# First attention of a two-block transformer kernel: bias row inside the keys, output projection and two value units among the heads, identity transposes in TensorE's waits

## The reference, cut to what matters

```python
u = rms_norm(h, norm_mix[0]); m = rms_norm(mem, norm_mem[0])
mk, mv = split(m @ w_mem_kv[0])
q, k, v, f_logit, mq = split(u @ fox_w_in)        # 12 heads of 64; mq: 4 heads
q = rms_norm(q, g_q); k = rms_norm(k, g_k)        # per head
c = cumsum(log_sigmoid(f_logit + b_f))
s = q @ k.T / 8 + (c[t] - c[s]);  s = where(causal, s, -1e30)
mix = softmax(s) @ v                              # forget ("fox") attention
mem_out = softmax(rms_norm(mq) @ rms_norm(mk).T / 8) @ mv
h = h + concat(mix, mem_out) @ fox_w_out          # 1024 x 1024
h = h + swiglu(rms_norm(h))                       # FFN
```

## Time and profile before

| | |
|---|---|
| time, median of 3 runs | 1890.23 us (1889.27 to 1890.61) |
| the profiled execution | 1889.91 us |
| its span, first to last instruction | 1888.1 us |
| PE busy | 1796.5 us (95%) |
| DVE / ACT / POOL busy | 77% / 62% / 11% |
| share of the chain that ended last | PE 85%, DVE 6%, ACT 5%, issue 2% |
| mean granted PE clock | 0.988 |

### The profile page before, as it was taken

The page is one execution under the profiler, slowest core; times in us unless marked ns, Lnnn a source line. Parts: engine busy times, 40 slices in busy tenths (PEclk is TensorE's granted clock), DMA queues, the critical chain, the costliest instruction groups (busy, mean ns, idle before and its releaser), DMA issues.

```text
span 1888.1 us, 27534 instructions
## 1 busy us (share of the span) xinstructions
PE 1796.5 (95%) x10586; PEld 1578.9 (84%) x10586; DVE 1446.0 (77%) x1327; ACT 1169.4 (62%) x1135; POOL 207.5 (11%) x161
## 2 busy tenths in 40 slices
PE   6988999999999999999999999999999999689997
PEld 5977999999878878788787887878877888589997
DVE  6765877779768888888888888888889854765554
ACT  5535444356667777877777778787776734743332
POOL 2033111122020000000000000000015000302221
PEclk8999999999999999999999999999999999899999
DMA  9604688841259999999999999999999933035540
GB/s 395 244 23 146 232 335 329 315 184 55 112 219 383 378 363 385 348 402 373 368 387 359 389 385 362 379 358 394 377 356 410 369 112 135 1 135 179 182 154 23
DMA packets 74571, 520.84 MB, mean 276 GB/s; under 512 B 8064, under 2 KB 8192, under 8 KB 13952
## 3 DMA queue, kind: packets, MB, share of 16 engines
q1 hardware_dynamic: 73056, 514.02, 71.7%
q0 software_dynamic: 1440, 5.77, 0.8%
HBM read 504.02 MB, written 15.73 MB: 275 GB/s over the span
## 4 chain that ended last, share of the span: by engine, by line
PE 85%; DVE 6%; ACT 5%; issue 2%; DMA 1%; POOL 1%; ACTq 0%; DVEq 0%; SPq 0%
PE ps L1174 25%; PE ps L1176 25%; PE ps L1175 25%; DVE wl L1688 2%; PE ps L1197 1%; ACT wh L1048 1%; PE ps L1375 1%; PE ps L1543 1%; DMA raw<-in_experts 1%; PE ps L1305 1%; PE ps L1326 1%; DVE sqz L1681 1%; ACT L1059 0%; ACT L1048 0%; PE ps L1188 0%
## 5 line engine op out<-in xcount | busy, mean ns | idle before, releaser
L1688 DVE TENSOR_TENSOR wl<-raw,wh 128x2048 fp32r<-128x2048 f32 x446 | 1025.9, 2303 | 294.5 <-ACT wh L753 169.2
L1048 ACT ACTIVATE wh<-raw 128x2048 fp32r<-128x2048 f32 x336 | 643.2, 1918 | 180.2 <-PE ps L1176 177.0
L1174 PE MATMUL ps<-wh,xh 128*128 128x512 f32 (+1 forms) x1040 | 397.9, 383 | 8.9 <-DVE wl L1688 8.8
L1176 PE MATMUL ps<-wh,xl 128*128 128x512 f32 (+1 forms) x1040 | 390.1, 375 | 0.0
L1175 PE MATMUL ps<-wl,xh 128*128 128x512 f32 (+1 forms) x1040 | 389.7, 375 | 0.0
L1174 PE MATMUL ps<-xh,wh 128*128 128x256 f32 x1184 | 343.4, 290 | 25.1 <-DVE xl L1688 11.4
L1175 PE MATMUL ps<-xl,wh 128*128 128x256 f32 x1184 | 338.9, 286 | 0.0
L1176 PE MATMUL ps<-xh,wl 128*128 128x256 f32 x1184 | 338.6, 286 | 0.0
L753 ACT ACTIVATE wh<-raw 128x2048 fp32r<-128x2048 f32 x107 | 204.2, 1909 | 175.0 <-PE ps L1176 171.1
L1174 PEld LDWEIGHTS ps<-xh,wh 128*128 128x128 f32 x1184 | 231.3, 195 | 30.2 <-issue 23.8
L1174 PEld LDWEIGHTS ps<-wh,xh 128*128 128x128 f32 x1040 | 195.9, 188 | 49.8 <-DVE wl L1688 15.9
(11 more groups left out here) (292 smaller groups left out, 1927.9 us busy)
## 6 DMA issues: line engine op xcount, KB each, us to landing
raw<-in_experts SPq DMA_DIRECT2D x336, 1024.0 KB, 6.9
raw<-in_units SPq DMA_DIRECT2D x134, 1024.0 KB, 6.0
x_rows<-big SPq DMA_DIRECT2D x1, 6144.0 KB, 34.5
big<-x_rows SPq DMA_DIRECT2D x8, 512.0 KB, 8.2
y_rows<-big SPq DMA_DIRECT2D x7, 512.0 KB, 8.3
y_rows<-big SPq DMA_DIRECT2D x1, 2560.0 KB, 40.4
big<-in_mem SPq DMA_DIRECT2D x1, 1024.0 KB, 7.1
hT<-in_x SPq DMA_DIRECT2D x1, 1024.0 KB, 9.0
```

What stands on the lines that cost most here:

```text
L1048: act.activation(wh[:, p % SPL, :], raw[:, n % RAW, :], ACT.Copy).then_inc(sem("hi_ready"), 1)
L1174: mm(out_, lh, rh, start=start, stop=False, **kw)
L1176: return mm(out_, ll, rh, start=False, stop=stop, **kw)
L1688: return V.tensor_tensor(out_, whole, leading.bitcast(F32), ALU.subtract)
```

## The change

1. The bias goes into the keys. Row 64 of an even head's `kz`, and row 0 of an odd head's, were zero; two DMAs issued by POOL put -c there. The matching row of the queries holds ones: queries of odd heads go to a new buffer `q_odd`, and POOL sets rows with four memsets. The 24 matmuls of L1308, `selh` and its copy go away; a query unit is scaled with two 64x512 instructions.
2. The order of units becomes fq0 fk0 fq1 fk1 fq2 fk2 fv0; fv1 and fv2 are multiplied in quarters (`values_half`) at steps 0 to 2 of the attention, and copied out by ACT at steps 2 and 3.
3. The output projection is stored by rows and added up in banks 4 to 7 as pairs finish: `fo_rows(g)`, 24 matmuls, at the even steps from 8 to 18, the last two behind the loop. Turned probabilities (bank 2) and pair outputs (bank 3) have one bank each now.
4. ACT copies turned probabilities first and takes exponentials after, and writes `xh` one step earlier; DVE's `xl` stays where it was. fo0 is split ahead of the attention, and `FOX_SPLITS` puts the splits of fo1, fo2, fo3 and of the first two FFN units at steps 6, 9, 11, 15 and 19.
5. PE transposes the identity into an unused bank at five waits (16, 16, 20, 20 and 20 times) and 12 times ahead of each pair in stick-breaking.

```diff
-UNITS_A = (["mk0", "mv0", "mq0"] + [f"{w}{j}" for w in ("fq", "fk", "fv") for j in range(3)]
+PROJ = ["fq0", "fk0", "fq1", "fk1", "fq2", "fk2", "fv0"]
+UNITS_A = (["mk0", "mv0", "mq0"] + PROJ + ["fv1", "fv2"]
...
-        selh = sqz[:, 0:FOX_HEADS * P].rearrange("p (h m) -> p h m", h=FOX_HEADS)
-        negc = sqz[:, FOX_HEADS * P:FOX_HEADS * P + T]
+        q_odd = view(0, FOX // P, T, sqz)
+        negc = plan_f[:, :, :].rearrange("p a b -> p (a b)")
...
-        FOX_SPLITS = {16: ("fv0",), 20: ("fv1", "fv2")}
+        FOX_SPLITS = {6: ("fv1",), 9: ("fv2",), 11: ("fo0",), 15: ("fo1",), 19: ("fo2",)}
...
-        add_attention(fox_maps)
+        add_attention(fox_maps, (2,), (3,))
         for j in range(4):
-            product(f"fo{j}", j)
-        S.add("nsum2", 6)
+            product(f"fo{j}", 4 + j)
+        S.add("nsum2", 3)
+        S.add("idle_ffn0", 2, own_signal=True, own_drain=True)
...                                                # POOL
+            pool.memset(q_odd[0:1, :, :], 1.0).then_inc(sem("queries_one"), 1)
+            pool.wait_ge(sem("queries_one"), 2)
+            pool.wait_ge(sem("negc_ready"), 1)
+            pool.wait_ge(sem("rows_zeroed"), 32)
+            for odd in range(2):
+                pool.dma_start(kz[HD * (1 - odd):HD * (1 - odd) + 1, odd:FOX_HEADS:2, :],
+                               negc[odd:FOX_HEADS:2, :]).then_inc(sem("bias_rows"), 16)
...                                                # ACT
+                    if 0 <= i - T_LAG < n:
+                        turned_out(a0 + i - T_LAG)
+                    if i < n and turned_first:
+                        exponentials(a0 + i)
+                    if 0 <= i - out_lag < n and (i - out_lag) % 2 == 1 and maps[a0]["kind"] != "diff":
+                        g = (a0 + i - out_lag) // 2
...
+            attention(fox_maps, beside_fox, out_lag=PV_LAG, turned_first=True)
...                                                # PE
+            def keep_running(name, n):
+                claim(pe, name)
+                for _ in range(n):
+                    pe.transpose(bank(name)[:, 0:P], ident, ident)
...
                             ins = mm(s[:, at:at + nk], m["q"][:, P * t:P * t + P], m["k"][:, 0:nk],
-                                     start=True, stop=not fox)
-                            if fox:
-                                ins = mm(s[:, at:at + nk], selh[:, m["head"], :], negc[:, 0:nk],
-                                         start=False, stop=True)
+                                     start=True, stop=True)
...
+            def fo_rows(g):
+                name, k = f"fo{g // 2}", g % 2
...
+                h, l = weights(name, 2)
                 wait_drained(pe, f"pv{g}")
-            for j in range(4):
-                by_channels(f"fo{j}")
+                for o in range(KT):
+                    n = slice(P * o, P * o + P)
+                    ins = exact(bank(f"fo{o // 2}")[:, T * (o % 2):T * (o % 2) + T], (h[:, k, n], l[:, k, n]),
+                                (xh[:, g, :], xl[:, g, :]), g == 0 and o % 2 == 0, g == KT - 1, skip_group_check=True)
...
+            def beside_fox(i):
+                if i == 0:
+                    values_half("fv1", 0)
+                if i == 1:
+                    values_half("fv1", 1)
+                    values_half("fv2", 0)
+                if i == 2:
+                    values_half("fv2", 1)
+                if i % 2 == 0 and i >= 8:
+                    fo_rows((i - 8) // 2)
...
+            fo_rows(KT - 2)
+            fo_rows(KT - 1)
             norm_sum(2)
+            keep_running("idle_ffn0", 20)
...                                                # stick-breaking
+                    claim(pe, f"sbx{i}")
+                    if i % 2 == 0:
+                        for _ in range(12):
+                            pe.transpose(x[:, 0:P], ident, ident)
                     pe.wait_ge(sem("sb_masked"), 2 * (i + 1))
-                    claim(pe, f"sbx{i}")
...                                                # DVE
+                elif asked[:2] == "fq":
+                    two = slice(2 * int(at), 2 * int(at) + 2)
+                    qk_scale(asked, [(qT[0:HD, two, :], 0, HD, gq8[:, 0:1]), (q_odd[HD:P, two, :], HD, P, gq8[:, 0:1])])
...
-            if j < 2:
-                split_after(f"fo{j}")
-            split_after("fo2")
```

More of the change, by code:

```diff
@@ L358, in build @@
         S.add("foxf", 2)
+        S.add("idle_x", 6, own_signal=True, own_drain=True)
         product("mq0", 3)
[L360 to L369, removed]
+        for n, (name, b) in enumerate(zip(PROJ, (7, 0, 1, 2, 3, 6, 7))):
+            product(name, b)
+            asked = (["mq0"] + PROJ)[n]
+            if asked in QK_UNITS:
+                k = QK_UNITS.index(asked)
+                S.add(f"qsum{k}", 4 + k % 2)
+            if n == 0:
+                S.add("cum", 6)
+        product("fv1", 4)
+        product("fv2", 7)
         maps = []
@@ L859, in _, with attention, exponentials, turned_out @@
                                    scale=-1.0).then_inc(sem("negc_ready"), 1)
[L860 to L863, removed]
             warm(ACT.Exp)
-            def attention(rng, meanwhile=None, before=None):
+            def attention(rng, meanwhile=None, before=None, out_lag=PV_LAG + 1, turned_first=False):
                 n, a0 = len(rng), rng[0]
+                def exponentials(a):
+                    w0, w1 = (P, 3 * P) if maps[a]["kind"] != "mem" else (T, 2 * T)
+                    act.wait_ge(sem("att_max"), 2 * (a + 1))
+                    for t, (lo, hi) in enumerate(((0, w0), (w0, w1))):
+                        act.activation(att_p[:, a % 3, lo:hi], att_p[:, a % 3, lo:hi], ACT.Exp,
+                                       bias=nmx[:, a % 3, t:t + 1],
+                                       accum_out=ssum[:, a % 3, t:t + 1]).then_inc(sem("att_exp"), 1)
+                def turned_out(a):
+                    w = 3 * P if maps[a]["kind"] != "mem" else 4 * P
+                    wait_filled(act, f"pT{a}")
+                    if a >= 2:
+                        act.wait_ge(sem("att_pv"), a - 1)
+                    act.activation(att_pT[:, a % 2, 0:w], bank(f"pT{a}")[:, 0:w],
+                                   ACT.Copy).then_inc(drained(f"pT{a}"), 1)
                 for i in range(n + PV_LAG + 1):
@@ L870, in attention @@
                         before(i)
[L871 to L878, removed]
-                    if 0 <= i - T_LAG < n:
[L880 to L888, removed]
+                    if i < n and not turned_first:
+                        exponentials(a0 + i)
+                    if 0 <= i - T_LAG < n:
+                        turned_out(a0 + i - T_LAG)
+                    if i < n and turned_first:
+                        exponentials(a0 + i)
+                    if 0 <= i - out_lag < n and (i - out_lag) % 2 == 1 and maps[a0]["kind"] != "diff":
+                        g = (a0 + i - out_lag) // 2
                         act.wait_ge(sem("att_pv"), 2 * (g + 1))
@@ L1798, in _ @@
             split_after("mq0")
[L1799 to L1800 removed]
+            for j, name in enumerate(PROJ):
+                split_after(name)
+                asked = (["mq0"] + PROJ)[j]
+                at = asked[2]
                 if j == 0:
```

137 lines of the change are left out of this document (93 added, 44 removed).

## The result

The changed kernel takes 1894.11 us (median of 10 runs, 1892.41 to 1896.24), the kernel before 1889.30 (1888.84 to 1891.77): a ratio of 1.0021 (95% interval 1.0012 to 1.0030), some 4 us slower. The profiled execution took 1893.85 with a span of 1891.7, 3.6 more than before.

A forecast was written before the change was run, and what follows sets the result against it. PE carries 85% of the chain, but the attention goes at the pace of a loop through four engines. Terms +1.3 + 3.7 - 1.8 - 1.3 - 3.6 - 1.3 = -3.0 from 1889.9, plus 0.3 for the median: 1887.2 us, range 1879.5 to 1893.5.

The forecast's parts named there:

- Bias row: First attention: 24 bias matmuls go, 7.8 us less PE work, none of it on the path while the loop sets the pace.
- Start and waits of the loop: First attention: PE's idle time goes from 11.1 to 20.4 us; with 7.8 less work, net +1.5, taken as +1.3.
- Clock inside the attention: Half clock behind the attention's long holes costs 1.25 us for each of three stretches: +3.7, between 0 and 6.9.
- Fills: Identity transposes in PE's waits: -1.8 us for the first two, -1.3 for the third, -3.6 for the later two, -1.3 in stick-breaking.
- Nothing in between: From the first FFN unit to 1515 both kernels run the same list, so their distance should stay constant.
- Rival C: Attention's half clock falls on PE's work between holes: four stretches of 2.3, 9.2 in place of 3.7; 1894.4 us; chance 0.09.
- A: Rival: the clock holds in the attention (+1.3) and the fills work fully (-11.1); 1880.4 us; chance 0.26.
- Rival B: The transposes in PE's waits don't hold the clock, so all fills drop out: +5.0, 1895.2 us; chance 0.07.
- D: Rival: the attention's holes are short, so idle time and bias partly leave the path: -9.5, fills -8.0, 1872 us; chance 0.06.

The follow-up runs named there:

- e5: The kernel before with the bias row alone (24 bias matmuls away, query units scaled in two instructions): 1890.66 us, ratio 1.0001.
- e9: e5 with 5 identity transposes ahead of PV at each of steps 4 to 15: 1891.19 us, ratio 1.0003 to the kernel before.
- e4: The changed kernel with PE kept busy in the attention's waits by transposes and matmuls that add zero: 1886.32 us, ratio 0.9971 to the kernel before.
- e3: The changed kernel with DVE's low part of a weight one step later than ACT's high part: 1877.92 us, ratio 0.9923 to the kernel before.
- e8: e7 with all fills longer (34, 30, 34, 34, 34 and 20 a pair): 1869.96 us, ratio 0.9897 to the kernel before.
- e2: The kernel before with the identity transposes alone, at the same places and counts: 1886.29 us, ratio 0.9974.
- e1: The changed kernel with none of the identity transposes: 1898.24 us, ratio 1.0035 to the kernel before.
- e6: e3 with matmuls of the old bias's size and place back in the fox heads' scores, adding zero: 1879.21 us, ratio 0.9933 to the kernel before.
- e7: e3 with 16 transposes ahead of the scores of step 2 and 14 ahead of PV at step 6: 1872.67 us, ratio 0.9899 to the kernel before.

## Why the prediction was wrong

The forecast was -3.0 us, with a chance of 0.11 for slower by more than 0.2%, and 1894.1 lies outside the range, by 0.6. In the profiled executions the span grew by 3.6. By the steps of the forecast:

- **Bias row** (7.8 us off PE, nothing of it on the path of the old loop): right as far as e5 and e9 show: the attention stayed at 88.2 against 88.4, though with stretches of half clock in both.
- **Start and waits of the loop** (idle time 11.1 to 20.4; net +1.5, +1.3 taken): the mechanism was right. Measured idle time is 17.9, net 6.7 - 7.8 = -1.1, which is 2.4 less than was taken; e4, less what is left of half clock in it, has an attention within 0.1 us of the kernel before. Single waits: 2.45 (2.0 said), 2.07 (2.4), 4.06, 3.12 and 3.32 (4.0), 2.01 (2.3). The mechanism of the three long ones is shown by e3.
- **Clock inside the attention** (three stretches of 1.25, +3.7): this is the step that failed. It measured 8.5 by busy time and 7.5 by e4, about 4 to 5 us above the term. Two things were sized wrongly. I counted only the waits of 3.5 us and more, though the earlier trace rows had one of 2.53 with half clock behind it; the waits of 2.45 and 2.07 were followed by it too, and one stretch lasted 6.7 us, so there were 20 us at half clock in place of 10. And I let a part of each fall on waits: PE was busy for 19.4 of the 20.2 us in them, so that a stretch of 3.4 cost 1.7.
- **Fills**: the second term that was off, by some 3.4 us in all (-4.6 measured, -8.0 said). -1.36 behind `norm_sum(2)` (-1.3 said); -3.25 from `norm_sum(5)` to `norm_sum(6)`, which holds the wait behind `norm_sum(5)` and stick-breaking (-1.9 - 1.3 said); -0.6 behind `norm_sum(6)` (-1.7 said), where one of two stretches stayed. At the first two waits nothing came back where -1.8 was said (`norm_sum(1)` starts 0.4 us later, the last sum per head 0.6): at 40 the clock had fallen before the transposes began, and at 20 sixteen were too few; e8 with 34 and 30 has both at full clock and `norm_sum(1)` 1.7 us earlier than in the changed kernel.
- **Nothing in between**: the distance grew by 0.9 us between `norm_sum(3)` and `norm_sum(5)`. The memory attention of the second layer has two stretches of half clock (498 and 542) where it had one (534), with the same instructions. That was not in the forecast.

The pieces add up: 0.6 up to the last sum per head, 7.35 in the attention, -1.36, +0.94, -3.25 and -0.61 make +3.7. The clock is the largest miss, and the waits that came out shorter than forecast hid a part of it.

Rival C gave 9.2 for the clock in the attention and 1894.4 in all, 0.3 us from the measurement; its sum left out the 0.3 of the median that A and B have, and with it is 1894.7. Its mechanism (half clock on work between two waits, so that it counts in full) is what the rows show, though not its stretch at step 19. That its total comes so near is luck in part: its attention is 3.1 us too long (10.5 against 7.35), while its fills give back 1.4 too much and the 0.9 in between isn't in it. It got a chance of 0.09, by the argument that half of the time around steps 9 to 16 is waiting. The rows say why that was wrong: the lower clock follows a wait and falls on the work behind it. The same could be read in the earlier trace rows, where PE was busy in all of 19.5 to 22.7, 43.5 to 46.8 and 194 to 197, though not in the two rows at 1518 and 1686. Rival B of the prediction (the fills hold nothing) has fallen with e2, A (no half clock in the attention) with the rows above, D (short holes) with the waits of 3.1 to 4.1 us. The Trainium skill's sentence on transposes ("TensorE: Matmul & The Clock Gate", Part 4: PE-mode transpose) does not hold in these runs: the wait behind `norm_sum(2)` is followed by half clock in e1, without transposes, and by 1.00 in the changed kernel with 20 and in e8 with 34.

## What to carry to other kernels

Price a wait of TensorE at its length plus half of the time at half clock that falls on work behind it; here the five stretches cost some 8 us, more than the 6.7 of added waiting. Look for such waits in the rows well below the longest: in these runs waits of 1.7 to 2.5 us were followed by half clock in some places and not in others. Where two engines split a job between them, let the second do its part a step after the first: DVE's wait for ACT sat in front of everything else that DVE owed, and moving it by one step was worth 18.5 us, over four times what the whole change had moved. Taking work off an engine that waits in a loop brought nothing here (e5); the same work taken off once the waits were gone was worth about 3 us in the profile (e6). The engine's waits can instead be filled with work from elsewhere: with the late split, the attention of the changed kernel is 10.2 us shorter than the old one, and 13.3 with full clock (e7).

## What was not expected of the hardware

Half clock came behind waits of 2.07 and 2.45 us inside an otherwise busy loop, but not behind one of 2.01 (191.23) nor behind 1.91 (201.88). The length alone doesn't tell, though: it came behind 2.02 (181.90 in e4), 1.97 (1691.56) and, in e5, behind 1.68 (120.61). One wait of 2.12 us is the same in the kernel before, where the clock stays at 1.00 behind it, and in e5, where it falls:

```profile
156.81 0.62 PE L1326 MATMUL ps<-att_pT,big 128*64 128x256 f32 x2 [2.12 <-ACT att_pT L885]
```

```profile
154.92 0.62 PE L1336 MATMUL ps<-att_pT,big 128*64 128x256 f32 x2 [2.12 <-ACT att_pT L899]
```

The prediction, which named only the wait of 0.87 us in the old loop, had passed over it.

Transposes of the identity kept the clock at 1.00 through waits of 4.1 us (e8). Why the clock had fallen at 40 us in the changed kernel and not in e8, with the same 12-column matmuls (3.64 us) ahead of both fills, stays open; in e4, with the same instructions up to there as the changed kernel, the stretch was half as long. And with an equal list of instructions the memory attention of the second layer had one such stretch (before), two (changed) or as much as three (e4: 3.4 and 6.8 us), so that a microsecond or two of any comparison here is where waits happen to fall.
